# Low halves of the expert blocks made by VectorE between the steps of a top-k choice, and one-hot tiles made two groups ahead

## The reference, cut to what matters

```python
v1, i1 = lax.top_k(s1, PEER_TOPK)
v2, i2 = lax.top_k(s2, PEER_TOPK)
cand = (v1[..., :, None] + v2[..., None, :]).reshape(T, PEER_HEADS, PEER_TOPK * PEER_TOPK)
vals, pos = lax.top_k(cand, PEER_TOPK)
experts = jnp.take_along_axis(cand_idx, pos, axis=-1)
gates = jax.nn.softmax(vals, axis=-1)
...
a = jnp.einsum('cd,chkd->chk', xc, u).astype(jnp.float32)
w = (jax.nn.gelu(a) * gc).astype(xc.dtype)
return jnp.einsum('chk,chkd->cd', w, expert_v[ec])
```

## Time and profile before

| | |
|---|---|
| median of 3 runs | 1766.71 us |
| the profiled execution's own time | 1768.2 us |
| its span in the trace | 1766.4 us |
| TensorE busy | 1704.1 us (96%) |
| VectorE busy | 1296.8 us (73%) |
| ScalarE busy | 962.0 us (54%) |
| GpSimd busy | 422.8 us (24%) |

### The profile page before, as it was taken

The page is one execution under the profiler, slowest core; times in us unless marked ns, Lnnn a source line. Parts: engine busy times, 40 slices in busy tenths (PEclk is TensorE's granted clock), DMA queues, the critical chain, the costliest instruction groups (busy, mean ns, idle before and its releaser), DMA issues.

```text
span 1766.4 us, 29535 instructions
## 1 busy us (share of the span) xinstructions
PE 1704.1 (96%) x10472; PEld 1504.1 (85%) x10472; DVE 1296.8 (73%) x2527; ACT 962.0 (54%) x1557; POOL 422.8 (24%) x186
## 2 busy tenths in 40 slices
PE   9999999988888888899999999999999999999998
PEld 8997999987777777788888888886899988989997
DVE  7658759985566566578887888777769975769984
ACT  6578654545555555553333333557566655556654
POOL 1220177786666666630000000000000000000000
PEclk9999999999999999999999999999999999999999
DMA  8661555566655655667777788663465565535562
GB/s 307 204 226 49 200 171 194 190 185 187 181 179 180 191 179 179 189 224 241 244 241 239 239 307 296 221 224 108 145 219 190 192 203 167 179 120 187 195 201 74
DMA packets 120448, 346.45 MB, mean 196 GB/s; under 512 B 13328, under 2 KB 45200, under 8 KB 118928
## 3 DMA queue, kind: packets, MB, share of 16 engines
q1 hardware_dynamic: 118480, 336.70, 58.5%
q10 hardware_dynamic: 1856, 8.23, 1.3%
HBM read 321.03 MB, written 23.86 MB: 195 GB/s over the span
## 4 chain that ended last, share of the span: by engine, by line
PE 83%; DVE 12%; ACT 3%; issue 1%; DMA 0%; ACTq 0%; DVEq 0%
PE banks L867 56%; PE bank L867 25%; DVE wsplit L2723 3%; DVE bank L2718 1%; DVE hot_a L2721 1%; DVE gates L2730 1%; DVE pick L2632 1%; DVE pick L2641 1%; PE bank L1271 0%; DVE act_e L2709 0%; DVE ropeg L2709 0%; ACT ropeg L2026 0%; ACT act_e L2026 0%; DVE pick L2615 0%; DVE pick L2637 0%
## 5 line engine op out<-in xcount | busy, mean ns | idle before, releaser
L867 PE MATMUL banks<-HT,wsplit 128*128 128x256 f32 (+1 forms) x3628 | 445.7, 284 | 3.2 <-POOL wsplit L1650 2.5
L867 PEld LDWEIGHTS banks<-HT,wsplit 128*128 128x128 f32 x3628 | 434.0, 190 | 12.8 <-issue 6.0
L1960 ACT ACTIVATE wsplit<-raw 128x1024 fp32r<-128x1024 f32 x252 | 266.7, 1058 | 213.1 <-PE banks L867 201.0
L867 PE MATMUL banks<-wsplit,wexp 128*128 128x512 f32 x1536 | 348.3, 389 | 0.0
L1650 POOL TENSOR_TENSOR wsplit<-raw,wsplit 128x1024 fp32r<-128x1024 f32 x124 | 305.3, 2465 | 144.7 <-ACT wsplit L1960 144.7
L867 PEld LDWEIGHTS banks<-wsplit,wexp 128*128 128x128 f32 x1536 | 288.2, 188 | 59.8
L867 PE MATMUL bank<-HT,wsplit 128*128 128x512 f32 (+1 forms) x1728 | 313.2, 338 | 0.0
L867 PEld LDWEIGHTS bank<-HT,wsplit 128*128 128x128 f32 x1728 | 271.2, 190 | 36.1
L1673 ACT ACTIVATE wsplit<-raw 128x1024 fp32r<-128x1024 f32 x146 | 154.3, 1059 | 97.4 <-PE bank L867 49.1
L2141 DVE TENSOR_TENSOR wsplit<-raw,wsplit 128x1024 fp32r<-128x1024 f32 x124 | 151.6, 1235 | 68.4 <-ACT wsplit L1673 67.1
L2703 DVE TENSOR_TENSOR wsplit<-raw,wsplit 128x1024 fp32r<-128x1024 f32 x128 | 156.1, 1220 | 1.1 <-ACT wsplit L1960 1.1
(11 more groups left out here) (335 smaller groups left out, 2147.7 us busy)
## 6 DMA issues: line engine op xcount, KB each, us to landing
raw<-weights SPq DMA_DIRECT2D x148, 512.0 KB, 4.1
raw<-expert_v SPq DMA_DIRECT2D x128, 512.0 KB, 3.5
raw<-expert_u SPq DMA_DIRECT2D x124, 512.0 KB, 3.7
raw1b<-weights SPq DMA_DIRECT2D x102, 512.0 KB, 4.2
raw1a<-weights SPq DMA_DIRECT2D x48, 512.0 KB, 4.2
HT<-acts_parked SPq DMA_DIRECT2D x124, 128.0 KB, 3.4
acts_parked<-act_e SPq DMA_DIRECT2D x62, 128.0 KB, 3.7
acts_parked<-ropeg SPq DMA_DIRECT2D x62, 128.0 KB, 3.7
```

The costliest lines, as they stand in the source:

```text
L867: ins = pe.matmul(out, lhsT, rhs, start=start, stop=stop, **kw)
L1960: act.activation(wsplit[:, s, 0, :], src, ACT.Copy).then_inc(e_hi, 1)
```

## The change: what it does

`EARLY` goes from 20 to 16, so `BULK` from 108 to 112, and `HOT_SPAN` from 104 to 108. The low halves of blocks 3 to 16 are made by VectorE (`second_part_of_u`, semaphore `u_lo_v`), each put between two steps of the choice; GpSimd makes 0 to 2 and 17 to 127. `u_made(n)` names the semaphore and the count for block n, and every wait for a low half of u uses it. The product of 8192 elements is cut into three, and the first sum of the tree into two. In the bulk, the one-hots of groups 0 and 1 are made before the loop, and in block m those of group g+2 are made in front of the sum of block m, where g is the group that stands at m.

```diff
-EARLY = 20
+EARLY = 16
+U_BY_VECTOR = range(3, 17)
-FIRST_HOT, HOT_SPAN = 2, 104
+FIRST_HOT, HOT_SPAN = 2, 108
+        def u_made(n):
+            if n in U_BY_VECTOR:
+                return u_lo_v, n - U_BY_VECTOR.start + 1
+            return u_lo, n + 1 - (len(U_BY_VECTOR) if n >= U_BY_VECTOR.stop else 0)
...
             for n in range(RAW, NKEYS):
-                sp.wait_ge(u_lo, n - 2 if n >= RAW + 3 else u_slot(n) + 1)
+                sp.wait_ge(*u_made(n - 3 if n >= RAW + 3 else u_slot(n)))
...
             for n in range(NKEYS):
+                if n in U_BY_VECTOR:
+                    continue
                 pool.wait_ge(e_hi, n + 1)
...
+            def second_part_of_u(n):
+                dve.wait_ge(e_hi, n + 1)
+                dve.tensor_tensor(wsplit[:, u_slot(n), 1, :], u_raw(n), f32(wsplit[:, u_slot(n), 0, :]),
+                                  ALU.subtract).then_inc(u_lo_v, 1)
...
+                for third, (j0, j1) in enumerate(((0, 6), (6, 11), (11, TOPK))):
...
+                    ins = dve.tensor_tensor(o4, o4, choices..., ALU.mult)
+                    second_part_of_u(9 + third)
...
+            for g in range(2):
+                make_hots(g)
             for m in range(BULK):
+                for g in hot_groups_at(m):
+                    if g + 2 < HOT_GROUPS:
+                        make_hots(g + 2)
                 add_halves(m)
                 for g in hot_groups_at(m):
                     gates_out(g)
-                for g in hot_groups_at(m + FIRST_HOT):
-                    make_hots(g)
```

More of the change, by code:

```diff
@@ L479, in block_stack @@
         e_hi, u_lo, v_lo = sem("expert_hi_made"), sem("u_lo_by_pool"), sem("v_lo_by_vector")
+        u_lo_v = sem("u_lo_by_vector")
         a_parked = [sem(f"acts_parked{s}") for s in range(4)]
@@ L791, in _ @@
                 else:
-                    sp.wait_ge(u_lo, (0, NKEYS - 1, NKEYS, NKEYS - 2)[e])
+                    sp.wait_ge(*u_made((0, NKEYS - 2, NKEYS - 1, NKEYS - 3)[e]))
                 load_v(e, e, v_block(e))
@@ L1456, in _ @@
                 b = open_bank(("ua", n))
-                pe.wait_ge(u_lo, n + 1)
+                pe.wait_ge(*u_made(n))
                 w = tiles_of(lambda part: wsplit[:, u_slot(n), part, :], k=KD)
@@ L1470, in times_u @@
             def times_u(m):
-                pe.wait_ge(u_lo, m + EARLY + 1)
+                pe.wait_ge(*u_made(m + EARLY))
                 if m >= 2:
@@ L2000, in _ @@
                 first_part_of_u(n + 3)
-                if n == 12:
+                if n == 10:
                     act.wait_ge(norm_d, KD * (TURNS.index("mem1") + 1))
@@ L2010, in _ @@
             act.activation(eT_parts[:, 2, :], bank(("et", 2))[:, 0:S], ACT.Copy).then_inc(et_hi, 1)
-            act.wait_ge(u_lo, RAW)
+            act.wait_ge(*u_made(2))
+            act.wait_ge(*u_made(RAW - 1))
             act.wait_ge(x_parked, 16)
@@ L2612, in pick_positions @@
                     ins = dve.tensor_copy(ptab[:, 1 + a], by_rank(tab[:, a, :].rearrange("p (t h k) -> p t h k", t=T, k=TOPK)))
+                second_part_of_u(3)
                 for s in range(2):
@@ L2619, in pick_positions @@
                 link(dve.scalar_tensor_tensor(out=row, in0=eighth, scalar=5.0, in1=fourth, op0=ALU.add, op1=ALU.max))
+                second_part_of_u(4)
                 link(dve.scalar_tensor_tensor(out=row, in0=p, scalar=-42.0, in1=row, op0=ALU.add, op1=ALU.max))
@@ L2623, in pick_positions @@
                 link(dve.tensor_scalar(fourth, row, 4.0, 24.0, ALU.mult, ALU.add))
+                second_part_of_u(5)
                 link(dve.scalar_tensor_tensor(out=start, in0=row, scalar=16.0, in1=eighth, op0=ALU.mult, op1=ALU.min))
@@ L2633, in pick @@
                                             ALU.is_equal)
+                    if j in (1, 8, 15):
+                        second_part_of_u(6 + j // 7)
                 link(ins)
[L2635 to L2638, removed]
+                for third, (j0, j1) in enumerate(((0, 6), (6, 11), (11, TOPK))):
+                    o4 = onehot16[:, j0:j1, :].rearrange("p j (a k h) -> p (j a) k h", k=TOPK, h=PEER_HEADS)
+                    choices = i16b[:, j0:j1, :, :, :].rearrange("p j s t h -> p (j s t) h")
+                    ins = dve.tensor_tensor(o4, o4, choices.unsqueeze(2).to_broadcast([P, (j1 - j0) * 2 * T, TOPK, PEER_HEADS]), ALU.mult)
+                    second_part_of_u(9 + third)
+                link(ins)
+                for j in (0, 4):
+                    ins = dve.tensor_tensor(onehot16[:, j:j + 4, :], onehot16[:, j:j + 4, :], onehot16[:, j + 8:j + 12, :], ALU.add)
+                    second_part_of_u(12 + j // 4)
+                link(ins)
+                n = 8
                 while n > 2:
@@ L2641, in pick @@
                     link(dve.tensor_tensor(onehot16[:, 0:n, :], onehot16[:, 0:n, :], onehot16[:, n:2 * n, :], ALU.add))
+                    if n == 4:
+                        second_part_of_u(14)
                 for s in range(2):
@@ L2647, in pick @@
                 link(ins)
+                second_part_of_u(15)
             def top16(values, spare, v, ix):
@@ L2687, in _ @@
                               gsum[:, 1, :, :].unsqueeze(2).to_broadcast([P, T, TOPK, PEER_HEADS]), ALU.mult).then_inc(ex_done, 1)
+            second_part_of_u(16)
             dve.wait_ge(et_hi, 1)
@@ L2692, in _ @@
             dve.wait_ge(iota_made, 1)
-            dve.wait_ge(u_lo, RAW)
+            dve.wait_ge(*u_made(2))
+            dve.wait_ge(*u_made(RAW - 1))
             dve.wait_ge(x_parked, 16)
```

## The result

The changed kernel took 1706.53 us (median of 4 runs, 1706.42 to 1706.68), against 1768.98 us for the kernel before (4 runs, 1765.05 to 1771.58): the ratio is 0.9649, 95% interval 0.9627 to 0.9671. Forecast were 1704 us and a range of 1699 to 1726. The profiled execution took 1706.52 us, with a span of 1704.7.

A forecast was written before the change was run, and what follows sets the result against it. TensorE was taken as the limit, held up by VectorE's late one-hots in the bulk and its choice. Profiled 1768.2 less 62.7 gives 1705.5 us, less 1.5 above the median a forecast of 1704 us, range 1699 to 1726.

The forecast's parts named there:

- Where the time was: In the bulk, TensorE waits 40 times for VectorE's last one-hot, 1.38 us each including slower gate products.
- The choice's own work: Ahead of the bulk, VectorE's choice takes 20.2 us without GpSimd, against 62 before, and ends at 363.2 us.
- Low halves ahead of TensorE: In the early blocks, VectorE's low halves are ready before TensorE wants them; tightest margin 1.0 us, nothing charged.
- The start of the bulk: At the first bulk blocks, TensorE waits 1.0 us for block 0's sum; the first two blocks gain 1.6 to 1.8 us.
- The bulk: All 40 waits go; the bulk takes 344.2 us and ends at 712.6 instead of 775.26, 62.7 us less.
- The slots: In the bulk, a slot turns over in 7.4 us, 8.6 with the longest landing, within 8.85 for three blocks.
- Rival (a): In the bulk, later loads make TensorE wait for GpSimd's low half; 1723 us at a 6 us landing; chance 0.10.
- The clock: TensorE's granted clock stays at 1.00 throughout, without the drop seen after the idle stretch before the bulk.
- rival (d): TensorE is granted a clock of 0.67 in part of the bulk; 1792 us with half of the blocks; chance 0.01.
- The sum: Whole kernel: profiled 1768.2 less 62.7 gives 1705.5 us; as that execution was 1.5 above the median, 1704 us.

## Why the prediction was right, step by step

- *Where the time was.* Confirmed. The one-hots alone are 55.1 us, the sum had 40 x 1.38 = 55.2 less the new wait.
- *The choice's own work.* Predicted end 363.2 us, measured 362.7. The product was put at 4.3 us, measured 4.42 in one piece; the compares at 0.285 us each, measured nearer 0.2 from start to start, since neighbours overlap. The end comes out right in part by luck: such overlaps made the chain shorter than its sum, and 2.5 us of waits for ScalarE, put at nothing, made it longer. VectorE then waited for ScalarE instead, first at block 9 (1.38 us), earlier than block 14 as predicted. The end of the early stage was set by TensorE: 368.1 against 368.4.
- *Low halves ahead of TensorE.* Confirmed: no gap in 336 products. The smallest margin by the rows above is that of block 3: its low half is there at 328.40, and TensorE wants it at about 329.8.
- *The start of the bulk.* The right mechanism, mis-sized: 1.46 us against 1.0. The sum of block 0 began at 375.03 us, as forecast (375.1), but TensorE wanted it at 374.14 instead of 374.5, and started at 375.60, 0.14 us after the sum's end. The first two blocks took 5.84 us where the kernel before took 7.38 in the same view, 1.5 us less; 1.6 to 1.8 were forecast.
- *The bulk.* 345.3 us from 368.07 to 713.35, against 344.2: 0.46 from the wait, 0.25 from the slower block behind it (3.04 us), which the sum left out, and the rest from blocks that took 2.79 to 2.80 us. Neither the sums nor the gates were late.
- *The slots.* Rival (a) did not come about; the margin of 0.25 us that the forecast gave it, at the longest landing, left out the time that a low half has to spare before TensorE wants it. No run made the turn itself longer, so how near it is to binding stays open.
- *The clock.* The granted clock was 1.00 in all stretches above, with TensorE busy almost without a break; rival (d) did not come about. The experiment with GpSimd making all shows the other side: in TensorE's pause of 13.4 us it falls to 0.70 and then 0.50 (the lower of its two levels, 1.2 instead of 2.4 GHz), and it is back at 1.00 from 386 us on, 5 us after work began.
- *The sum.* The own time was forecast at 1705.5 us and is 1706.5. The larger part of the miss of 2.5 us in the median is the last step, the 1.5 us by which the profiled execution lay above the median of three runs. That was scatter of the kernel before (1765 to 1772 us in all groups), which the changed kernel does not have (1706.4 to 1706.8). The 62.7 us were read from that same execution, so its excess was very likely already among what the change removes, and was subtracted twice. The runs point to the choice as its place: with only the one-hots as before, ten executions lie within 0.3 us (1764.73 to 1765.04), while with only the choice as before four of them spread over 1.9 us (1711.92 to 1713.79). Why was not tried.

## What to carry to other kernels

When a consumer waits again and again for the last of several small operations of a helper engine, compute from the order how long before the need it starts: making it one step earlier in the queue or one buffer further ahead each removed 44 waits, and doing both brought nothing more. Prologues count: what is prepared ahead of a loop stands in front of the loop's first result. And before a small chain on VectorE is trimmed, look whether GpSimd runs beside it; 14 instructions of 1.22 us added to the chain made it end 18 us earlier than leaving them to GpSimd.

## What the runs showed of the hardware

A GpSimd low half costs VectorE's chain of bf16 steps one turn of 2.2 to 2.4 us each, whatever the step's own length: a compare of 278 ns takes 2507 ns, and the product of 4.42 us takes 6.63. A float32 subtraction with two SBUF inputs waited too (3.40 instead of 1.22 us). The one-hots of the bulk, with one operand in a bank, never did (1215 to 1216 ns in all 64 of the changed kernel, beside a busy GpSimd). Unexpected was that blocks coming every 3.08 instead of 3.60 us, at 214 instead of 182 GB/s, left the median landing of a load of 512 KB at 3.7 us.
